# Token transposes in pieces and contraction tiles of contiguous channels at the beginning of a hybrid mixer and MoE block

## The reference

```
h = x * rsqrt(mean(x*x) + EPS) * norm_mix
z = h @ w_in                         # (256, 2048) @ (2048, 11296)
... gated DeltaNet and GLA mixers on columns of z, merge, w_out, residual ...
x = x + hier_moe(rmsnorm(x, norm_ffn), ...)
y = rmsnorm(x, norm_final)
```

## Time and profile before

| | us |
|---|---|
| median of 3 runs | 1760.34 |
| lowest, highest | 1759.96, 1762.64 |
| span of the profiled execution | 1758.5 |
| TensorE busy in it | 1694.6 |
| first matmul of chunk 0 | 12.32 |
| first matmul of chunk 1 | 18.33 |

### The profile page before, as it was taken

How to read it: one execution, slowest core, us unless ns; L and a number is a source line. 1 busy time by engine, 2 the same in 40 slices (tenths; PEclk the granted TensorE clock), 3 DMA queues, 4 the chain that set the end, 5 groups by cost and what they waited for, 6 DMA issues and landing times.

```text
span 1758.5 us, 23736 instructions
## 1 busy us (share of the span) xinstructions
PE 1694.6 (96%) x10116; PEld 1103.1 (63%) x10116; DVE 673.3 (38%) x772; ACT 425.2 (24%) x462; POOL 183.6 (10%) x249
## 2 busy tenths in 40 slices
PE   8999999999999999999999999999999999999996
PEld 7998989988888788887444443444344433443442
DVE  5356778646854546533122220222022202220222
ACT  6344445225533433333100000000000000000002
POOL 5000042410240200000000000000000000000001
PEclk9999999999999999999999999999999999999999
DMA  8455435434542655649999999999999999999997
GB/s 258 155 171 168 158 131 190 126 118 144 168 145 97 187 182 189 218 166 420 424 414 428 427 429 429 429 428 429 428 428 429 428 429 429 429 428 427 427 427 295
DMA packets 96071, 537.59 MB, mean 306 GB/s; under 512 B 5804, under 2 KB 5868, under 8 KB 70012
## 3 DMA queue, kind: packets, MB, share of 16 engines
q1 hardware_dynamic: 95408, 535.85, 76.8%
q0 software_dynamic: 592, 0.69, 0.3%
HBM read 534.42 MB, written 2.10 MB: 305 GB/s over the span
## 4 chain that ended last, share of the span: by engine, by line
PE 73%; DMA 22%; DVE 2%; ACT 1%; issue 1%; SPq 1%; POOL 0%; DVEq 0%; ACTq 0%; POOLq 0%
DMA arena<-in_w 22%; PE psum L2167 13%; PE psum L2192 10%; PE psum L1656 9%; PE psum L1657 9%; PE psum L1658 9%; PE psum L2082 4%; PE psum L1675 3%; PE psum L1676 3%; PE psum L1677 3%; PE psum L2210 1%; PE psum L2209 1%; PE psum L1905 1%; PE psum L2123 1%; PE psum L1911 0%
## 5 line engine op out<-in xcount | busy, mean ns | idle before, releaser
L2167 PE MATMUL psum<-arena 128*64 128x512 f32 x2048 | 458.5, 605 | 35.0 <-DMA arena<-in_w 34.2
L2167 PEld LDWEIGHTS psum<-arena 128*64 128x64 f32 x2048 | 147.9, 139 | 334.7 <-issue 285.8
L1099 DVE TENSOR_TENSOR w_lo<-arena,w_hi 128x2048 fp32r<-128x2048 f32 x119 | 277.8, 2338 | 186.8 <-ACT w_hi L769 186.6
L769 ACT ACTIVATE w_hi<-arena 128x2048 fp32r<-128x2048 f32 x119 | 227.6, 1914 | 267.9 <-PE psum L1658 196.9
L1656 PE MATMUL psum<-w_hi,hT_hi 128*128 128x512 f32 x568 | 228.1, 402 | 0.1
L1657 PE MATMUL psum<-w_lo,hT_hi 128*128 128x512 f32 x568 | 225.3, 397 | 0.0
L1658 PE MATMUL psum<-w_hi,hT_lo 128*128 128x512 f32 x568 | 225.3, 397 | 0.0
L2192 PE MATMUL psum<-arena 128*64 128x512 f32 x960 | 212.3, 599 | 4.9 <-DMA arena<-in_w 4.9
L2192 PEld LDWEIGHTS psum<-arena 128*64 128x64 f32 x960 | 67.5, 138 | 138.4 <-issue 126.3
L1675 PE MATMUL psum<-hT_hi,w_hi 128*128 128x256 f32 x512 | 146.0, 285 | 0.0
L1677 PE MATMUL psum<-hT_hi,w_lo 128*128 128x256 f32 x512 | 144.9, 283 | 0.0
(11 more groups left out here) (404 smaller groups left out, 1478.7 us busy)
## 6 DMA issues: line engine op xcount, KB each, us to landing
arena<-in_w SPq DMA_DIRECT2D x186, 2048.0 KB, 26.2
arena<-in_w_in SPq DMA_DIRECT2D x87, 1024.0 KB, 5.0
arena<-in_w_out SPq DMA_DIRECT2D x16, 1024.0 KB, 5.0
arena<-in_w SPq DMA_DIRECT2D x10, 1024.0 KB, 23.4
arena<-in_w_oa SPq DMA_DIRECT2D x8, 1024.0 KB, 5.0
arena<-in_w_ob SPq DMA_DIRECT2D x8, 1024.0 KB, 5.0
arena<-in_x SPq DMA_DIRECT2D x4, 1024.0 KB, 6.9
arena<-in_w SPq DMA_DIRECT2D x4, 512.0 KB, 15.4
```

Source lines behind the costliest of these rows:

```text
L769: nc.scalar.activation(w_hi[x % NSPLIT], ringA[:, x % RING_A, :], ACT.Copy).then_inc(sem("w_hi"), 1)
L1099: tt(w_lo[x % RING_A], ringA[:, x % RING_A, :], w_hi[x % NSPLIT].bitcast(F32), ALU.subtract)\
L2167: i = mm(bank(w)[e * CAP:(e + 1) * CAP, :], xeT[:, k, e * CAP:(e + 1) * CAP], rows, start=(k == 0), stop=(k == KT - 1))
```

## The change

The channel tiles are made of contiguous channels: tile k holds the channels k*128 + p, in `win_v` and in the tokens. The tokens are loaded as four pieces of 512 columns of both halves (512 KB each), each ahead of the chunk of weights that needs it. TensorE transposes a piece at a time: pieces 0 and 1 ahead of chunk 0, piece 2 ahead of chunk 1, piece 3 ahead of chunk 2. The PSUM banks of the pairs are 4, 5, 6, 7, 2, 3, 4, 5, so that banks 0 and 1 are free for chunk 0. The norm weight is loaded as 16 rows of 128, transposed by TensorE into bank 1 and copied by DVE. The identity transposes are 14 instead of 18. Two semaphores are shared with others (`b_rf` with `b_ms`, `small_t` with `small_split`).

```diff
-    win_v = w_in[0].rearrange("(p k) n -> p k n", k=KT)
+    win_v = w_in[0].rearrange("(k p) n -> p k n", p=P)
...
+        nmix_rows = rdiag[0:KT, 0:P]
...
+        def token_bank(i):
+
+            return bank((4, 5, 6, 7, 2, 3, 4, 5)[i])
...
-            sp.dma_start(xs0[:, 0, :], x_v[:, 0, :]).then_inc(sem("x_in0"), 16)
-            sp.dma_start(nmix, norm_mix[0].rearrange("(p k) -> p k", k=KT)).then_inc(sem("nmix_in"), 16)
-            sp.dma_start(xs0[:, 1, :], x_v[:, 1, :]).then_inc(sem("x_in1"), 16)
+            def load_tokens(piece):
+
+                cs = slice(piece * CB, (piece + 1) * CB)
+                sp.dma_start(xs0[:, :, cs], x_v[:, :, cs]).then_inc(sem(f"x_in{piece}"), 16)
+
+            load_tokens(0)
+            sp.dma_start(nmix_rows, norm_mix[0].rearrange("(k p) -> k p", p=P)).then_inc(sem("nmix_in"), 16)
...
                 for h in range(1 if b == 0 else 0, BCH):
+                    if b == 0:
+                        load_tokens(h)
                     load(x, win_v[:, h * CT:(h + 1) * CT, c:c + CB])
...
-            act.wait_ge(sem("nmix_in"), 16)
+            act.wait_ge(sem("nmix_in"), 18)
...
-            dve.wait_ge(sem("nmix_in"), 16)
+            dve.wait_ge(sem("nmix_in"), 17)
+            nc.vector.tensor_copy(nmix, bank(1, KT)).then_inc(sem("nmix_in"), 1)
+            dve.wait_ge(sem("nmix_in"), 18)
...
-            keep_running(18)
-            for m in range(NM):
-                pe.wait_ge(sem(f"x_in{m}"), 16)
-                for i in range(8):
+            keep_running(14)
+            pe.wait_ge(sem("nmix_in"), 16)
+            tr(bank(1, KT), nmix_rows, ident[0:KT, 0:KT]).then_inc(sem("nmix_in"), 1)
+
+            def transpose_tokens(piece):
+
+                pe.wait_ge(sem(f"x_in{piece}"), 16)
+                for i in (2 * piece, 2 * piece + 1):
                     for k in range(2):
-                        j = tr(bank(i)[:, (k * NM + m) * P:(k * NM + m + 1) * P], xs0[:, m, 2 * i + k::KT], ident)
-                    if m == NM - 1:
-                        j.then_inc(sem("xTp"), 1)
+                        for m in range(NM):
+                            at = (2 * i + k) * P
+                            j = tr(token_bank(i)[:, (k * NM + m) * P:(k * NM + m + 1) * P], xs0[:, m, at:at + P],
+                                   ident)
+                    j.then_inc(sem("xTp"), 1)
+
+            transpose_tokens(0)
+            transpose_tokens(1)
...
             for x in range(1, FIRST_BLOCKS * BCH):
+                if x + 1 < BCH:
+                    transpose_tokens(x + 1)
                 if x < BCH:
                     wait(pe, ("hTl", 2 * x + 2))
                 project(x)
```

More of the change, by code:

```diff
@@ L366, in drained @@
                 return "attn_tmp", (1 if base == "lv_eye" else LEVELS.index(int(base[2:])) + 2)
-            alias = {"small": "small_t", "smallT": "zs", "o": "a_o", "bo0": "b_o", "bo1": "b_o", "obT0": "obT", "obT1": "obT",
+            alias = {"small": "small_split", "smallT": "zs", "o": "a_o", "bo0": "b_o", "bo1": "b_o", "obT0": "obT", "obT1": "obT",
                      "ssq": "ssqk", "S": "a_S", "kd": "kdtok", "gc": "gate_cols", "oi": "inter", "gkT": "gkx"}
@@ L372, in drained @@
                 return "A", 2 * g + 1
-            n = {"bo1": 2, "obT1": 2, "gc": 2}.get(base, 1)
+            n = {"bo1": 2, "obT1": 2, "gc": 2, "small": 3}.get(base, 1)
             return alias.get(base, base), g + n
@@ L638, in _ @@
             wait(pool, ("b_ms", 1))
-            nc.gpsimd.tensor_tensor(rmf[:, 0:8], rms[:, 0:8], pw[:, 0:8], ALU.pow).then_inc(sem("b_rf"), 1)
+            nc.gpsimd.tensor_tensor(rmf[:, 0:8], rms[:, 0:8], pw[:, 0:8], ALU.pow).then_inc(sem("b_ms"), 1)
             def diagonal_blocks(dst, m):
@@ L799, in high_tokens @@
                 for k in range(2):
-                    j = nc.scalar.activation(hTh[:, 2 * i + k, :], bank(i)[:, k * SEQ:(k + 1) * SEQ], ACT.Copy,
+                    j = nc.scalar.activation(hTh[:, 2 * i + k, :], token_bank(i)[:, k * SEQ:(k + 1) * SEQ], ACT.Copy,
                                              scale=nmix[:, 2 * i + k:2 * i + k + 1])
@@ L829, in _ @@
             nc.scalar.activation(T_["bo"][0:NSM, 0:SEQ], pair("small")[0:NSM, 0:SEQ], ACT.Copy)\
-                .then_inc(sem("small_t"), 1)
+                .then_inc(sem("small_split"), 1)
             result("smallT")
@@ L1110, in low_tokens @@
                 for k in range(2):
-                    j = stt(hTl[:, 2 * i + k, :], bank(i)[:, k * SEQ:(k + 1) * SEQ], nmix[:, 2 * i + k:2 * i + k + 1],
+                    j = stt(hTl[:, 2 * i + k, :], token_bank(i)[:, k * SEQ:(k + 1) * SEQ], nmix[:, 2 * i + k:2 * i + k + 1],
                             hTh[:, 2 * i + k, :].bitcast(F32), ALU.mult, ALU.subtract)
                 j.then_inc(sem("hTl"), 1)
-            dve.wait_ge(sem("nmix_in"), 16)
+            dve.wait_ge(sem("nmix_in"), 17)
+            nc.vector.tensor_copy(nmix, bank(1, KT)).then_inc(sem("nmix_in"), 1)
+            dve.wait_ge(sem("nmix_in"), 18)
             low_tokens(0)
@@ L1267, in _ @@
             ts(rms[:, 0:8], rms[:, 0:8], 1.0 / B_DV, EPS, ALU.mult, ALU.add).then_inc(sem("b_ms"), 1)
-            wait(dve, ("b_rf", 1))
+            wait(dve, ("b_ms", 2))
             o3 = T_["bo"].rearrange("p (u e) -> p u e", u=8)
@@ L1698, in _ @@
             pe.wait_ge(sem("ident"), 1)
-            keep_running(18)
-            for m in range(NM):
-                pe.wait_ge(sem(f"x_in{m}"), 16)
-                for i in range(8):
-                    for k in range(2):
-                        j = tr(bank(i)[:, (k * NM + m) * P:(k * NM + m + 1) * P], xs0[:, m, 2 * i + k::KT], ident)
-                    if m == NM - 1:
-                        j.then_inc(sem("xTp"), 1)
+            keep_running(14)
[4 more added lines that the diff above has]
+                for i in (2 * piece, 2 * piece + 1):
+                    for k in range(2):
+                        for m in range(NM):
[5 more added lines that the diff above has]
+            transpose_tokens(1)
             for half in range(2):
+                wait(pe, ("hTl", half + 1))
                 for m in range(NM):
-                    if half == 0:
-                        wait(pe, ("hTl", m + 1))
                     if m == 0:
@@ L1741, in _ @@
             fill("cw")
-            wait(pe, ("small_t", 1))
+            wait(pe, ("small_split", 3))
             for m in range(NM):
```

## The result

The changed kernel takes 1764.75 us in the median of 12 runs (1763.77 to 1766.87), the kernel before 1762.12 in 12 (1759.96 to 1763.14). The ratio is 1.0021, with an interval of 1.0013 to 1.0028: **slower by 0.2%**, between 2.3 and 4.9 us. The medians are 2.6 us apart, the ratio stands for 3.7; both lie in that interval. The prediction was 1761.2 with a range up to 1764.0, and no difference that could be told. Its direction was that of the forecast, its size was not: the time lies above the range.

The account below looks back on a forecast made before the run. TensorE was taken to bound the kernel until 820 us, expert weights after. Chunk 3's delay (-2.7 + 2.0 + 2.0 - 0.5 = +0.85 us) moves the end: 1758.5 + 0.85 + 1.84 = 1761.2 us, range 1758.9 to 1764.0.

Parts of the forecast that it names:

- What bounds the kernel: TensorE sets the pace to 820 us, then expert weights; the end moves as does the moment TensorE stops waiting, before 30 us.
- Part 1: Token and weight landings, transposes, ACT and DVE up to chunk 0: it starts at 9.6 us, 2.7 us earlier than before.
- the second token piece at 8.4: Landing of piece 1 in the load queue: at 8.4 us, from the 2048 KB ahead of it.
- rates not near 390 GB/s: Sign that the prediction is wrong: DMA rates from 2 to 18 us not near 390 GB/s.
- The DVE copy of the norm weight: DVE ahead of chunk 0: between zero and 1.23 us, lower end taken; at the upper end it would cost 0.2 us.
- The clock: Rival: TensorE at the lower clock around chunk 0, first matmuls 0.43 us apart, all 1.8 us later, 1763.0 us; chance 0.15.
- Part 2: Eight transposes before chunk 1 and eight before chunk 2, 1.0 us each time; chunk 1 at 16.3, chunk 2 at 22.9.
- Part 3: Chunk 3 waits about 2 us for tokens 6 and 7, square, split and DVE; it starts at 30.5, before 29.65.
- The sum: Chunk 0 -2.7, transposes +2.0, wait before chunk 3 +2.0, gap ahead of chunk 1 -0.5: +0.85 us, giving 1761.2 us.
- the base: The time before the change in the forecast: the profiled run of 1758.5 us plus 1.84 to the median of the runs.
- The range: 1758.9 to 1764.0 us, holding the forecast, the case without a chunk 3 wait, most of the clock rival, 0.5 us scatter.
- The forecast of chunk 4: Its split is done by DVE at 35.1, TensorE asks at 36.1; GpSimd's small loads are untouched, so nothing more is lost.

Follow-up runs that it names:

- section 6: Five probes that change only the loads of the kernel before (e3, e6, e7, e11, e12); single runs of 1763.3, 1762.8, 1762.8, 1764.9 and 1766.2 us.
- e2: The changed kernel with 16 more identity transposes on TensorE between token pieces 0 and 1; 1763.15 us, ratio 1.0010 to the kernel before.
- e1: The changed kernel with ACT's square of the first token half moved behind the split of chunk 3; 1764.18 us against 1761.88 before, ratio 1.0016.
- e5: The changed kernel with the edits of e1 and e2 together; 1761.97 us against 1761.22 for the kernel before, ratio 1.0002.
- e6: The kernel before with each token half loaded in two transfers of 512 KB with runs of 2 KB; 1762.8 us in one run.
- e3: The kernel before with each token half loaded in four transfers of 512 columns (runs of 2 KB); 1763.3 us in one run.
- e12: The kernel before with chunk 0's weights issued first, then each token half in four transfers of 512 columns; 1766.2 us in one run.
- e4: The changed kernel with tokens loaded as two halves ahead of the weights, all 32 transposes ahead of chunk 0, 18 identity transposes; 1761.37 us, ratio 1.0001 to before.
- e11: The kernel before with the two halves of chunk 0's weights issued ahead of whole token halves; 1764.9 us in one run.
- e7: The kernel before with each token half loaded in two transfers of 512 KB with runs of 4 KB; 1762.8 us in one run.
- e8: The changed kernel with two token pieces of 1024 columns, 16 transposes ahead of chunk 0 and 16 behind, and e1's late square; 1761.74 us, ratio 1.0002 to before.
- e9: e5 with ACT's copy of the small weights moved behind the split of chunk 4; 1761.18 us against 1761.53 for the kernel before, ratio 0.9998.
- e10: e8 with the small weights copied behind the split of chunk 4 and 18 identity transposes; 1761.48 us against 1761.53 before, ratio 0.9999.

## Why the prediction was wrong

**What bounds the kernel, right.** Of the 3.59 us at the marker, 3.42 have arisen by the start of chunk 3 at 33 us, and they pass on to the marker.

**Part 1, the start of chunk 0, wrong.** The step that failed is "the second token piece at 8.4 (the same 2048 KB ahead of it as for the second token row before)". It took equal bytes for equal time, with a rate from whole rows of 8 KB and from weight chunks, and no row had tokens in short runs. It landed at 10.04, 1.64 us late. That term was mis-sized by leaving out how the source is read; what in it makes the rate low stays open (section 6). The whole queue was late, by the times of issue and landing: piece 0 at 5.0 (forecast 4.5), the norm weight at 5.3 (4.5), the two halves of chunk 0's weights at 7.0 and 8.4 (5.8 and 7.1). The prediction had named this as a sign of being wrong, rates not near 390 GB/s between 2 and 18 us. The chain on ACT and DVE came 0.5 to 0.6 late as well: ACT took the first token pair at 6.79 (6.3), and DVE ended the first low half at 10.1 (9.4 to 9.5), which took 1.50 us where 1.23 before. Even with piece 1 at 8.4, chunk 0 would have started near 10.3 in this execution; in e2 DVE was done at 9.4. The DVE copy of the norm weight took 0.17 us and cost nothing.

**The clock, named and priced about right, but thought unlikely and left out of the sum.** I gave it 0.15 as a rival, and its sign, 0.43 spacing, came. e2 measures it: 1.56 us at the marker, against my 1.8. I counted with an idle time of 2.2 us; the late piece made it 2.73. That the late piece brought the low clock about is likely but not shown: no run had piece 1 at 8.4, and the length of the idle time doesn't settle the level (see the last section).

**Part 2, the moved transposes, right.** Eight took 1.0 us on TensorE, and cost 0.8 from the first transpose to the next chunk.

**Part 3, the wait before chunk 3, right.** From chunk 1 to chunk 3 it is 14.1 us, where the sum said 14.2, with a wait of 1.72 (about 2). e1 removed it.

**The sum.** Chunk 3 at 33.07 instead of 30.5 is 1.8 from a later start of chunk 0 (11.42 for 9.6, of which the slow transposes of piece 1 are some 0.5), 1.1 from chunk 0 at the slow clock, and -0.3 from moved transposes and chain: 2.6 in all. The forecast of chunk 4, "nothing more is lost", held in the changed kernel, but its ground, small loads "untouched here", did not: in e5 they landed 1.9 us later, which shows that this was a wait in hiding.

**The range and the base.** The range was made of cases, each alone; its upper end held the clock without the late piece. With both, the sum's own terms give 1761.2 + 2.6 = 1763.8, still inside it. The rest is the base. The sum starts from the median of 3 runs, 1760.34, and that of 12 runs is 1762.12, 1.8 us higher; the three are among the twelve. The number thus missed by 3.6 us for two reasons. By the medians they weigh the same: 1.8 for the base, and 1.8 for a difference of 2.6 us where 0.85 was forecast. From the base of 12 runs the same forecast would have been 1763.0. That the time lies above the range is in part this; that the difference is three to four times the forecast one is the late piece and the clock.

## What to carry to other kernels

A transfer cut into shorter runs is another transfer: its time is to be taken from a row with the same runs, the same number of transfers and the same source, not from bytes in the queue. A base of three runs that scatter by 2.7 us can be off by more than the effect; the sum should carry that. Work that is moved out of the idle beginning into the middle is paid in full by the engine that bounds the kernel, and every engine that consumes it in program order must be followed through to the step that the bounding engine needs next. When one rival makes another more likely (a later landing, a longer idle, a lower clock), price them together. Whether the later landing did bring the lower clock here is not shown; that both came is.

## What the runs showed of the hardware

**TensorE's clock at the start.** The granted clock stands at 1.00 in the profile from the first instruction, but transposes are 0.214 us apart at first and about 0.118 to 0.13 later; only the spacing shows the level there. In the changed kernel the eight transposes at 5.58 still took 1.73 us, in e1 the same eight took 1.09: the rise falls at a different moment from execution to execution.

The length of the idle time before it doesn't settle the level. In e6, the kernel before with other loads, TensorE idled only 1.82 us ahead of its first token transposes and 0.79 ahead of the second, and from 10 to 15 us the granted clock was at the lower level:

```profile
10.00:15.00 5.00, 4.03 (x18) 0.50 1.05 396
```

In e3 it idled 1.51 and 2.06 us there, and in the kernel before up to 1.89, and the granted clock stayed at 1.00; in e1 (3.86 us) and e12 (3.66 us) it was at 0.50 behind the wait.

**GpSimd beside DVE.** Six copies of 64 by 64 took 1.72 us before and 3.84 in the changed kernel. The same view of GpSimd, before:

```profile
14.32 1.72 POOL L603 COPY arena<-arena 64x64 f32<-64x64 f32 x6
```

and after:

```profile
13.82 3.84 POOL L614 COPY arena<-arena 64x64 f32<-64x64 f32 x6
```

They end at 17.66, shortly after DVE's low part of chunk 1, which ran from 14.68 to 16.97 across them; before, that DVE instruction started at 15.89, when the copies were almost done. The small loads are queued behind the copies, and their last one was issued at 25.73 instead of 24.11. No run changed it alone, but the other traces bear it out. The copies take 1.71 to 1.73 us in the four traces in which no such DVE instruction (a subtraction `w_lo`, two inputs in SBUF) lies across most of them (before, e3, e4, e12), 2.64 and 2.76 where one of 1024 columns and 1.23 us does (e11, e6), 3.62 with two of these (e7), and 3.67 to 3.87 where one of 2048 columns and 2.3 us does (the changed kernel, e1, e2, e5, e8, e9, e10). With one such instruction they get longer by its own time less 0.1 to 0.4 us.
